# Mixture-of-experts stage on one Trainium2 core: result rows stored from ScalarE's queue, gathers left alone on GpSimd

## Chip, cores, metric

The kernel runs on one core of a Trainium2 chip, in one launch. The metric is the device time of that launch in microseconds. Engines are named as in the profile: PE (TensorE), ACT (ScalarE), DVE (VectorE), POOL (GpSimd), SP (SyncE, here only issuing DMAs).

## What is computed

Two transformer-like blocks over 512 tokens of width 1024, all in float32: first a mixer (dilated attention beside gated linear attention) and a mixture of experts, then a second mixer (pooling beside an RWKV recurrence). The change touches the mixture of experts alone, cut here to what matters:

```python
logits = xt @ router_w + router_b                 # 512 tokens, 32 experts
top_v, top_i = lax.top_k(logits, 4)
gates = softmax(top_v)
# for each expert e and the tokens that chose it (xb = their rows):
gu = xb @ w_gate_up[e] + b_gate_up[e]             # 1024 -> 2 * 1024
x_glu = minimum(gu[:, ::2], 7); x_lin = clip(gu[:, 1::2], -7, 7)
act = x_glu * sigmoid(1.702 * x_glu) * (x_lin + 1)
out = act @ w_down[e] + b_down[e]                 # 1024 -> 1024
# y[token] = sum over its 4 experts of gate * out
```

## The kernel before

The program runs in stages, one block of engine programs each, with a barrier between: `stage_front`, `mixers`, `stage_router`, `stage_experts`, `stage_second`, `stage_rwkv`. The change is in `stage_experts`.

**Units.** The tokens of each expert are cut into units of 32 rows (`SLOTS`); an expert has at least one unit. The router stage leaves a table with each unit's expert and slot code, and the count of units. Every engine walks over the units in a loop (`Fori(1, units)`), the first unit being written out ahead of it. A unit's 32 rows of 1024 lie in SBUF as 128 x 256: four quarters of the columns on four groups of 32 partitions.

**Weights.** An expert has twelve chunks of 1 MB (128 x 2048 float32), eight of gate/up and four of down. SP issues them in order of the experts (line 1653) into 18 slots (`staging`, one and a half experts). Before each it waits till the chunk that held the slot 18 earlier is used by the last unit of its expert (`free`), and after each for the landing of the one issued four before (`arrived`, which raises `chunk_in`). A quarter of each chunk is read by PE from its slot; the other three quarters are copied into a ring of four places first, chunks 2, 5, 7 and 10 by ACT (line 1785), the others by DVE (line 1853). The copies are made anew for each unit.

**PE, in each step of the loop** (lines 1767 to 1772): gate/up of unit i (`up`, eight chunks), down of unit i - 1 (`down`, four chunks), the transposes of unit i's hidden tile (`turn_hidden`, line 1736), the transposes of the gathered rows of unit i + 2 (`turn_rows`, line 1704), and the bias of unit i + 1 (line 1714).

**ACT, in each step:** three ring fills (chunks 5, 7, 10), the gate, the copy of the transposed rows (`rows_turned`), the fill of chunk 2 for the next unit, then `read_y`, which copies the down result of unit i - 1 from PSUM to `y` (line 1808) once `y_free` says that `y` was stored, and then the copy of the transposed hidden tile (`hidden_turned`, line 1796).

**POOL, in each step** (lines 1690 to 1692): `gather(i + 2)`, which reads the slot code from the table, waits till the gather before has landed (`rows_in`) and till PE has transposed the rows of unit i + 1 (`rows_ps`; the tile `rows` has a single buffer), copies the slot numbers and issues the indirect DMA (line 1676); then `store_rows(i)`, which waits for `y_read`, issues the store of `y` to DRAM (line 1683), waits for its landing and raises `y_free`. The loop is in program order, so the next gather begins after the store has landed.

The last unit's result is stored by SP (line 1660).

Of the kernel before, what the change touches and what calls it, by code (L numbers as in the profile page):

```python
# [32 lines left out]
NE, TOPK = 32, 4  # L33
# [1502 lines left out]
def stage_experts(k):  # L1536

    nc, d = k.nc, k.d
    with ExitStack() as ctx:
# [27 lines left out]
        rows_in = sem("rows_in")  # L1567
        rows_ps = sem("rows_ps")
# [10 lines left out]
        y_read = sem("expert_y_read")  # L1579
        y_out = sem("expert_y_out")  # L1580
        y_free = sem("expert_y_free")
        last_out = sem("expert_last_out")
# [35 lines left out]
        def store_of(n):  # L1618
            return d["expert_rows"][bass.ds(n, SLOTS), :].rearrange("r (c n) -> c r n", c=QUARTERS)

        with nc.Block() as block:
            @block.sync
            def _(sp):
# [34 lines left out]
                end = sp.value_load(k.table[0:1, TABLE - 2:TABLE - 1], min_val=NE - 1, max_val=NBLK - 1)  # L1658
                sp.wait_ge(y_read, end + 1)
                sp.dma_start(store_of(end * SLOTS), y[:]).then_inc(last_out, 16)  # L1660
                sp.wait_ge(last_out, 16)

            @block.gpsimd
            def _(pool):
                units = units_on(pool)
                by_quarter = d["h2"].rearrange("t (c n) -> (t c) n", c=QUARTERS)

                def gather(i, out=rows, at=0):
                    code = pool.value_load(k.table[0:1, bass.ds(i + P, 1)], min_val=0, max_val=CODES - 1)
                    if out is rows:  # L1670
                        after(pool, rows_in, 16 * i)
                        after(pool, rows_ps, i)
                    pool.tensor_copy(slot[:, at:at + 1], k.slots[:, bass.ds(code, 1)]).then_inc(slot_ready, 1)  # L1673
                    pool.wait_ge(slot_ready, i + 1)
                    pool.sem_inc(slot_seen, 1)
                    pool.indirect_dma_start(  # L1676
                        out=out[:], out_offset=None, in_=by_quarter,
                        in_offset=bass.IndirectOffsetOnAxis(ap=slot[:, at:at + 1], axis=0)).then_inc(rows_in, 16)

                def store_rows(n):  # L1680

                    pool.wait_ge(y_read, n)
                    pool.dma_start(store_of(n * SLOTS - SLOTS), y[:]).then_inc(y_out, 16)  # L1683
                    pool.wait_ge(y_out, 16 * n)
                    pool.sem_inc(y_free, 1)

                gather(0, y, 1)
                gather(1)
                gather(2)
                with pool.Fori(1, units) as i:  # L1690
                    gather(i + 2)
                    store_rows(i)
                pool.wait_ge(rows_in, 16 * units + 32)

            @block.tensor
            def _(pe):
# [3 lines left out]
                def turn_rows(i, src=rows):  # L1700
                    pe.wait_ge(rows_in, 16 * i + 16)
                    after(pe, rowsT_ready, i)
                    for b in range(2):
                        mm = pe.transpose(k.bank(6)[:, b * P:(b + 1) * P], src[:, b * P:(b + 1) * P], ident)  # L1704
                    mm.then_inc(rows_ps, 1)
# [73 lines left out]
            def _(act):  # L1779
# [25 lines left out]
                def read_y(n, done):  # L1805
                    act.wait_ge(chunk_done, done)
                    act.wait_ge(y_free, n + 1)
                    act.activation(y[:], k.bank(4)[:, 0:GLU], ACT.Copy).then_inc(y_read, 1)  # L1808

                act.sem_inc(y_free, 1)  # L1810
# [16 lines left out]
                with act.Fori(1, units) as i:  # L1827
# [7 lines left out]
                    read_y(i - 1, i * CHUNKS + CHUNKS)  # L1835
                    hidden_turned(i)
# [6 lines left out]
                read_y(end, units * CHUNKS + CHUNKS)  # L1843

# [1275 lines left out]
```

## Time and profile before

| | us |
|---|---|
| median of 3 runs | 2101.05 |
| lowest and highest | 2095.19, 2104.95 |
| the profiled execution, its own time | 2098.68 |
| its span in the profile | 2097.1 |

In that span PE is busy for 81%, DVE for 54%, ACT for 41%, POOL for 12%; 516.46 MB are moved, 246 GB/s in the mean. The expert stage is the stretch from some 368 to some 1696 us.

Busy time is the time in which an engine executes; issuing DMAs, waiting and branching are not counted. A wait is put down to what released it. PE's granted clock is written as a share of 2.4 GHz, so that 0.5 is the level of 1.2 GHz.

### The profile page before, as it was taken

The numbers are of one execution on the slowest core, as the hardware profiler recorded it, in microseconds if no ns is written. First come the engines' busy times: TensorE is split into PE (matmuls) and PEld (weight loads), VectorE is DVE, ScalarE is ACT, GpSimd is POOL, SyncE is SP. The second block draws the span as 40 slices with busy tenths as digits, with TensorE's granted clock in tenths as the row PEclk, the third lists the DMA queues.
The fourth block names the chain that finished last, engine by engine and source line by source line (L and its number), as shares of the span: only waits on it lengthen the run. The fifth ranks groups of instructions, "written<-read, shape, count | busy, mean of one in ns | idle before, by whom it ended". The sixth has DMA issues, their size and how long they took to land. (4 is left out here: it accounts for less than half of the span.)

```text
span 2097.1 us, 50062 instructions
## 1 busy us (share of the span) xinstructions
PE 1704.3 (81%) x16925; PEld 894.4 (43%) x16926; DVE 1136.5 (54%) x1698; ACT 853.6 (41%) x1131; POOL 257.8 (12%) x304
## 2 busy tenths in 40 slices
PE   6999898677977787878887787879778657999797
PEld 4999644232332332323332233323323125777763
DVE  5874536554654554545654555546545356694555
ACT  5344521543543443434543444434444234442421
POOL 0000000211111111111111111111111030151000
PEclk9999998897998888989987889889988777999999
DMA  8871840659478866995389985997598983231011
GB/s 301 277 242 33 216 190 21 260 220 423 163 305 335 336 265 259 394 381 221 137 343 404 424 337 222 371 400 302 205 415 344 417 308 80 73 91 42 4 52 40
DMA packets 135287, 516.46 MB, mean 246 GB/s; under 512 B 19927, under 2 KB 58728, under 8 KB 85929
## 3 DMA queue, kind: packets, MB, share of 16 engines
q1 hardware_dynamic: 117016, 483.74, 58.9%
q0 software_dynamic: 18048, 31.20, 4.5%
q8 instruction: 51, 0.84, 0.2%
q10 hardware_dynamic: 146, 0.48, 0.1%
q14 instruction: 26, 0.21, 0.0%
HBM read 492.44 MB, written 22.81 MB: 246 GB/s over the span
## 5 line engine op out<-in xcount | busy, mean ns | idle before, releaser
L1853 DVE COPY ring<-staging 128x1536 f32 (+1 forms) x638 | 600.5, 967 | 578.0 <-PE banks L1727 464.3
L1785 ACT ACTIVATE ring<-staging 128x1536 f32 (+1 forms) x319 | 473.8, 1487 | 731.6 <-PE banks L1727 545.9
L1727 PE MATMUL banks<-staging,rowsT 128*32 (+1 forms) x1268 | 633.5, 654 | 42.4 <-DVE ring L1853 21.3
L1727 PE MATMUL banks<-ring,rowsT 128*32 128x512 f32 x3840 | 641.9, 655 | 0.0
L1727 PEld LDWEIGHTS banks<-staging,rowsT 128*32 128x32 f32 x1268 | 140.8, 118 | 480.8 <-issue 476.6
L1750 PE MATMUL banks<-staging,hiddenT 128*32 x1280 | 294.0, 383 | 1.6 <-DVE ring L1853 1.3
L1750 PE MATMUL banks<-ring,hiddenT 128*32 128x256 f32 x3840 | 294.8, 383 | 0.0
L1704 PE MATMUL banks<-sq,rows 128*128 128x128 f32 x162 | 41.1, 343 | 234.5 <-DMA rows<-h_rows,slot 234.5
L1750 PEld LDWEIGHTS banks<-staging,hiddenT 128*32 128x32 f32 x1280 | 141.7, 111 | 153.7 <-issue 47.3
L1750 PEld LDWEIGHTS banks<-ring,hiddenT 128*32 128x32 f32 x3840 | 155.3, 111 | 0.0
L1727 PEld LDWEIGHTS banks<-ring,rowsT 128*32 128x32 f32 x3840 | 155.2, 118 | 0.0
L602 PE MATMUL banks<-w_in_hi,hT 128*128 128x256 f32 (+1 forms) x768 | 147.3, 291 | 1.5 <-issue 1.5
L1673 POOL COPY slot<-slots 128x1 int32 x82 | 30.2, 368 | 878.5 <-issue 857.8
L2196 PE MATMUL banks<-h3T,w_in_hi 128*128 128x512 f32 x400 | 129.4, 405 | 1.4 <-DVE h3T L2374 1.4
L1704 PEld LDWEIGHTS banks<-sq,rows 128*128 128x128 f32 x162 | 21.0, 165 | 245.1 <-DMA rows<-h_rows,slot 245.1
L602 PEld LDWEIGHTS banks<-w_in_hi,hT 128*128 128x128 f32 x768 | 122.5, 194 | 3.5 <-issue 3.5
L1683 POOL DMA_DIRECT2D expert_rows<-y_rows x79 | 62.8, 795 | 388.6 <-ACT y_rows L1808 365.7
L602 PE MATMUL banks<-w_in_lo,hT 128*128 128x256 f32 (+1 forms) x384 | 109.7, 286 | 0.0
L1676 POOL DMA_INDIRECT rows<-h_rows,slot x81 | 96.4, 1190 | 66.6 <-POOL slot L1673 51.0
L2196 PEld LDWEIGHTS banks<-h3T,w_in_hi 128*128 128x128 f32 x400 | 76.1, 191 | 23.1 <-issue 4.1
L2196 PE MATMUL banks<-h3T,w_in_lo 128*128 128x512 f32 x200 | 78.9, 395 | 0.0
L602 PEld LDWEIGHTS banks<-w_in_lo,hT 128*128 128x128 f32 x384 | 74.5, 194 | 1.9 <-issue 1.9
(434 smaller groups left out, 1939.2 us busy)
## 6 DMA issues: line engine op xcount, KB each, us to landing
staging<-in_w_gate_up SPq DMA_DIRECT2D x250, 1024.0 KB, 11.5
staging<-in_w_down SPq DMA_DIRECT2D x128, 1024.0 KB, 12.8
stage<-in_w_mod SPq DMA_DIRECT2D x21, 1024.0 KB, 5.8
stage<-in_w_in SPq DMA_DIRECT2D x25, 512.0 KB, 4.0
stage<-in_w_in SPq DMA_DIRECT2D x11, 1024.0 KB, 6.1
expert_rows<-y_rows POOLq DMA_DIRECT2D x79, 128.0 KB, 8.6
expert_rows<-catT SPq DMA_DIRECT2D x1, 7936.0 KB
early<-in_w_gate_up SPq DMA_DIRECT2D x6, 1024.0 KB, 12.9
```

The source lines that it names most:

```text
L602: mm = pe.matmul(k.bank(4 + t)[:, 0:w], hT[:, a, q, tt], b[:, q, :], start=(q == 0 and a == 0 and b is hi), stop=(q == KT - 1 and a == 1))
L1673: pool.tensor_copy(slot[:, at:at + 1], k.slots[:, bass.ds(code, 1)]).then_inc(slot_ready, 1)
L1676: pool.indirect_dma_start(out=out[:], out_offset=None, in_=by_quarter, in_offset=bass.IndirectOffsetOnAxis(ap=slot[:, at:at + 1], axis=0)) ...
L1683: pool.dma_start(store_of(n * SLOTS - SLOTS), y[:]).then_inc(y_out, 16)
L1704: mm = pe.transpose(k.bank(6)[:, b * P:(b + 1) * P], src[:, b * P:(b + 1) * P], ident)
L1727: mm = pe.matmul(k.bank(0)[c * SLOTS:(c + 1) * SLOTS, :], rowsT[:, q % 2, row], w, start=first and q == 0, stop=not first and q == KT - 1, ...
L1750: mm = pe.matmul(k.bank(4)[c * SLOTS:(c + 1) * SLOTS, 0:GLU], hT[:, b, m * SLOTS:(m + 1) * SLOTS], w, start=(m == 0 and b == 0), stop=(m = ...
L1785: act.activation(ring[:, pos % RING, :], staged(i, e, pos, PART, CHUNK - PART), ACT.Copy).then_inc(act_filled, 1)
L1853: dve.tensor_copy(ring[:, pos % RING, :], staged(i, e, pos, PART, CHUNK - PART)).then_inc(dve_filled, 1)
L2196: mm = pe.matmul(k.bank(n % 4), w[:, n % NW, q, :], hT[:, b, q, :], start=(q == 0 and a == 0), stop=(q == KT - 1 and a == 2))
```

## The change

The store of `y` moves from POOL to ACT: after `read_y`, ACT waits for its own copy to be written (`y_read`) and issues the store from its own DMA queue; the copy for the next unit waits for that store's landing (`y_out`). The last store too is ACT's, and SP's is removed. POOL only gathers. It waits itself for the landing of each gather and then raises `rows_here`, on which PE now waits in place of `rows_in`; then it waits for the transposes of those rows and gathers the next into the same buffer. The first two gathers, into `y` and `rows`, have a semaphore each, and the second no longer waits for the first.

```diff
--- before.py
+++ after.py
@@ -1565,6 +1565,9 @@
         slot_ready = sem("slot_ready")
         slot_seen = sem("slot_seen")
         rows_in = sem("rows_in")
+        first_in = [sem(f"first_rows{m}_in") for m in range(2)]
+        rows_here = sem("rows_here")
+        rows_free = sem("rows_free")
         rows_ps = sem("rows_ps")
         rowsT_ready = sem("rowsT_ready")
         chunk_in = sem("chunk_in")
@@ -1577,9 +1580,8 @@
         turned_ps = sem("hidden_turned_ps")
         hT_ready = sem("hiddenT_ready")
         y_read = sem("expert_y_read")
+        y_seen = sem("expert_y_seen")
         y_out = sem("expert_y_out")
-        y_free = sem("expert_y_free")
-        last_out = sem("expert_last_out")
         settled = sem("early_settled")
         gate_diff = sem("gate_diff")
         gate_exp = sem("gate_exp")
@@ -1655,42 +1657,38 @@
                     arrived(m - AHEAD)
                 for m in range(NE * CHUNKS - AHEAD, NE * CHUNKS):
                     arrived(m)
-                end = sp.value_load(k.table[0:1, TABLE - 2:TABLE - 1], min_val=NE - 1, max_val=NBLK - 1)
-                sp.wait_ge(y_read, end + 1)
-                sp.dma_start(store_of(end * SLOTS), y[:]).then_inc(last_out, 16)
-                sp.wait_ge(last_out, 16)
 
             @block.gpsimd
             def _(pool):
                 units = units_on(pool)
                 by_quarter = d["h2"].rearrange("t (c n) -> (t c) n", c=QUARTERS)
 
-                def gather(i, out=rows, at=0):
+                def gather(i, out, at, done):
                     code = pool.value_load(k.table[0:1, bass.ds(i + P, 1)], min_val=0, max_val=CODES - 1)
-                    if out is rows:
-                        after(pool, rows_in, 16 * i)
-                        after(pool, rows_ps, i)
                     pool.tensor_copy(slot[:, at:at + 1], k.slots[:, bass.ds(code, 1)]).then_inc(slot_ready, 1)
                     pool.wait_ge(slot_ready, i + 1)
                     pool.sem_inc(slot_seen, 1)
                     pool.indirect_dma_start(
                         out=out[:], out_offset=None, in_=by_quarter,
-                        in_offset=bass.IndirectOffsetOnAxis(ap=slot[:, at:at + 1], axis=0)).then_inc(rows_in, 16)
-
-                def store_rows(n):
-
-                    pool.wait_ge(y_read, n)
-                    pool.dma_start(store_of(n * SLOTS - SLOTS), y[:]).then_inc(y_out, 16)
-                    pool.wait_ge(y_out, 16 * n)
-                    pool.sem_inc(y_free, 1)
-
-                gather(0, y, 1)
-                gather(1)
-                gather(2)
+                        in_offset=bass.IndirectOffsetOnAxis(ap=slot[:, at:at + 1], axis=0)).then_inc(done, 16)
+
+                gather(0, y, 1, first_in[0])
+                gather(1, rows, 2, first_in[1])
+                pool.wait_ge(first_in[0], 16)
+                pool.sem_inc(rows_here, 1)
+                pool.wait_ge(first_in[1], 16)
+                pool.sem_inc(rows_here, 1)
+                pool.wait_ge(rows_ps, 2)
+                pool.sem_inc(rows_free, 1)
+                gather(2, rows, 0, rows_in)
                 with pool.Fori(1, units) as i:
-                    gather(i + 2)
-                    store_rows(i)
-                pool.wait_ge(rows_in, 16 * units + 32)
+                    pool.wait_ge(rows_in, 16 * i)
+                    pool.sem_inc(rows_here, 1)
+                    pool.wait_ge(rows_ps, i + 2)
+                    pool.sem_inc(rows_free, 1)
+                    gather(i + 2, rows, 0, rows_in)
+                pool.wait_ge(rows_in, 16 * units)
+                pool.sem_inc(rows_here, 1)
 
             @block.tensor
             def _(pe):
@@ -1698,7 +1696,7 @@
                 ident = k.sq[:, IDENT, :]
 
                 def turn_rows(i, src=rows):
-                    pe.wait_ge(rows_in, 16 * i + 16)
+                    pe.wait_ge(rows_here, i + 1)
                     after(pe, rowsT_ready, i)
                     for b in range(2):
                         mm = pe.transpose(k.bank(6)[:, b * P:(b + 1) * P], src[:, b * P:(b + 1) * P], ident)
@@ -1804,10 +1802,15 @@
 
                 def read_y(n, done):
                     act.wait_ge(chunk_done, done)
-                    act.wait_ge(y_free, n + 1)
+                    act.wait_ge(y_out, 16 * n + 16)
                     act.activation(y[:], k.bank(4)[:, 0:GLU], ACT.Copy).then_inc(y_read, 1)
 
-                act.sem_inc(y_free, 1)
+                def store_y(n):
+                    act.wait_ge(y_read, n + 1)
+                    act.sem_inc(y_seen, 1)
+                    act.dma_start(store_of(n * SLOTS), y[:]).then_inc(y_out, 16)
+
+                act.sem_inc(y_out, 16)
                 rows_turned(0, 0)
                 fill(0, 0, 2)
                 act.wait_ge(bias_set, 1)
@@ -1833,6 +1836,7 @@
                     rows_turned(i + 1, i * CHUNKS + KT)
                     fill(i + 1, expert_on(act, i + 1), 2)
                     read_y(i - 1, i * CHUNKS + CHUNKS)
+                    store_y(i - 1)
                     hidden_turned(i)
                 act.wait_ge(act_filled, units * len(BY_ACT) + 1)
                 act.sem_inc(act_filled, 2)
@@ -1841,6 +1845,9 @@
                 act.activation(k.gates[:], k.gates[:], ACT.Exp).then_inc(gate_exp, 1)
                 end = act.value_load(k.table[0:1, TABLE - 2:TABLE - 1], min_val=NE - 1, max_val=NBLK - 1)
                 read_y(end, units * CHUNKS + CHUNKS)
+                store_y(end)
+                act.wait_ge(y_out, 16 * units + 16)
+                act.sem_inc(y_seen, 1)
 
             @block.vector
             def _(dve):
```

How instructions stand on POOL in the loop over the units, before: the table read, slot copy and gather, followed by the store (L1683).

```order
L1690 ISA
L1669 TENSOR_LOAD table
L1669 ISA x2
L1596 ISA
L1673 ISA
L1673 COPY slot<-slots 128x1
L1674 REGISTER_ALU
L1676 DMA rows<-h_rows,slot 128x256
L1683 ISA
L1683 DMA expert_rows<-y_rows 4x32x256
L1684 REGISTER_ALU
L1690 REGISTER_ALU
```

And with the change, the same loop on POOL; L1687 is the wait for the transposes.

```order
L1684 ISA
L1687 REGISTER_ALU
L1667 ISA
L1667 TENSOR_LOAD table
L1667 ISA x2
L1668 ISA
L1668 COPY slot<-slots 128x1
L1669 REGISTER_ALU
L1671 DMA rows<-h_rows,slot 128x256
L1684 REGISTER_ALU
L1684 COMPARE_AND_BRANCH
```

The store is gone from POOL's loop, and the table read, which stood ahead of the waits, now stands behind them.

On ACT, at the end of each step of the loop, the y copy, the hiddenT copy and the branch back, before:

```order
L1808 ACTIVATE y_rows<-banks 128x256
L1796 ACTIVATE hiddenT<-banks 128x256
L1827 REGISTER_ALU
L1827 COMPARE_AND_BRANCH
L1837 ISA
```

And with the change, the same place on ACT:

```order
L1805 ISA
L1806 ACTIVATE y_rows<-banks 128x256
L1811 ISA
L1811 DMA expert_rows<-y_rows 4x32x256
L1794 ACTIVATE hiddenT<-banks 128x256
L1830 REGISTER_ALU
L1830 COMPARE_AND_BRANCH
```

The store's issue now stands between the y copy and the hiddenT copy, and the fills of the next step come behind both.

## Rows read from the trace of the kernel before

**Rows 1.** The page's 40 equal slices of the span: PE busy, DMA share, GB/s

```profile
PE   6999898677977787878887787879778657999797
...
DMA  8871840659478866995389985997598983231011
GB/s 301 277 242 33 216 190 21 260 220 423 163 305 335 336 265 259 394 381 221 137 343 404 424 337 222 371 400 302 205 415 344 417 308 80 73 91 42 4 52 40
```

**Rows 2.** Busy time by stretch of the span, engine by engine (us, instructions in brackets)

```profile
core 0: us, PE busy (x) PEld busy (x) DVE busy (x) ACT busy (x) POOL busy (x), PEclk, DMA share, GB/s
395.25:1686.69 1291.44, 1019.52 (x10587) 390.76 (x10587) 666.29 (x871) 556.30 (x632) 184.32 (x236) 0.87 0.78 314
948.09:959.60 11.51, 11.51 (x138) 4.75 (x135) 8.48 (x12) 7.05 (x9) 0.76 (x1) 1.00 1.04 414
959.60:980.44 20.84, 13.10 (x138) 5.00 (x135) 8.34 (x12) 7.03 (x9) 3.46 (x5) 0.84 0.56 224
1004.75:1016.26 11.51, 11.51 (x138) 4.75 (x134) 8.47 (x12) 7.04 (x9) 2.62 (x3) 1.00 0.08 19
1016.26:1029.07 12.81, 11.80 (x138) 4.86 (x134) 8.35 (x12) 7.04 (x9) 2.44 (x3) 1.00 0.09 24
971.00:1031.00 60.00, 58.00 (x674) 23.67 (x666) 41.98 (x55) 35.19 (x40) 11.49 (x14) 1.00 0.08 24
1143.00:1204.00 61.00, 46.06 (x488) 17.71 (x484) 32.64 (x42) 26.66 (x31) 9.67 (x12) 0.84 1.01 425
```

**Rows 3.** Waits of PE between 395 and 1687 us: total us, times, longest

```profile
PE banks L1704 <- DMA rows<-h_rows,slot: 231.6, 39, 9.6
PE banks L1727 <- DVE ring L1853: 20.0, 17, 6.0
PE banks L1727 <- ACT ring L1785: 14.1, 11, 1.9
```

**Rows 4.** Timeline of POOL, 945 to 986 us: start, us, what, idle before and releaser

```profile
950.06 0.76 POOL L1683 DMA_DIRECT2D expert_rows<-y_rows  x1 [9.70 <-ACT y_rows L1808]
959.96 0.46 POOL L1673 COPY slot<-slots 128x1 int32 x1 [9.13 <-issue]
961.24 0.99 POOL L1676 DMA_INDIRECT rows<-h_rows,slot  x1 [0.82 <-ACT y_rows L1808]
```

**Rows 5.** Timeline of PE, 947 to 971 us: hidden tile (L1736), gathered rows (L1704)

```profile
948.37 0.38 PE L1704 MATMUL banks<-sq,rows 128*128 128x128 f32 x2
...
959.60 0.44 PE L1736 MATMUL banks<-sq,glu 128*128 128x128 f32 x2
967.68 0.69 PE L1704 MATMUL banks<-sq,rows 128*128 128x128 f32 x2 [7.64 <-DMA rows<-h_rows,slot]
```

**Rows 6.** Tile y_rows, whole program: the stores' landing

```profile
DMA to landing us min/median/max: 3.7/8.6/9.9
```

**Rows 7.** Tile rows, whole program: the gathers' landing

```profile
DMA to landing us min/median/max: 2.7/6.1/7.9
```

**Rows 8.** Line 1660: the last store, issued by SP (ns min/median/max)

```profile
L1660 SPq DMA_DIRECT2D expert_rows<-y_rows x1: 774/774/774, 1694.3 to 1694.3; - x1
```

**Rows 9.** Timeline of ACT, 0 to 12 us: a DMA issue of its own

```profile
4.46 0.50 ACTq L424 DMA_DIRECT2D mod<-in_b_mod  x1
```

**Rows 10.** Timeline of SP, 0 to 12 us: issues behind each other

```profile
1.83 5.53 SPq L418 DMA_DIRECT2D stage<-in_w_mod  x3
```

**Rows 11.** Timeline of ACT, 1003 to 1018 us: y copy (L1808), ring fill (L1785)

```profile
1005.64 0.37 ACT L1808 ACTIVATE y_rows<-banks 128x256 f32<-128x256 f32 x1
...
1008.02 1.49 ACT L1785 ACTIVATE ring<-staging 128x1536 f32 x1 [1.74 <-PE banks L1727]
```

**Rows 12.** DMA queues, 1143 to 1204 us: packets, MB, share of 16 engines

```profile
q1 hardware_dynamic: 3450, 25.12, 97.7%
```

**Rows 13.** Line 1653, 395 to 1690 us: the weight transfers' landing

```profile
DMA to landing us min/median/max: 4.7/12.0/15.1
```

## The prediction

> **What bounds the kernel now.** I read the page's slices first: PE is busy nearly throughout, the DMA engines swing between 1 and 9 tenths [rows 1]. In the expert stage neither is full. So I took the stage from the first to the last transposition of a hidden tile, 395.25 to 1686.69: 1291.4 us for 79 steps from unit to unit, PE busy 1019.5, clock 0.87, DMA share 0.78 [rows 2]. A step that waits for nothing takes 11.51 us, beside idle DMA engines (share 0.08) and beside full ones (1.04) alike [rows 2]; transfers in flight do not slow PE. 79 such steps are 909.3 us, so 382 us of the stage are something else. PE's own waits name the largest part: 231.6 us in 39 waits for gathered rows, against 20.0 + 14.1 us for weight copies into the ring [rows 3]. The other 116 us are spread over the steps with waits, 3.0 us for each of the 39. One shows how: 959.60 to 980.44 is 20.84 us = 11.51 + 7.64 of wait + 1.7, at granted clock 0.84, so partly at the 1.2 GHz level after the idle time. Another waited 0.30 us and still took 12.81 at full clock [rows 2].
>
> Why the rows are late is seen on POOL [rows 4] beside PE [rows 5]. The transposes that free rows run at 948.37. POOL cannot gather: it stores the result of an older unit at 950.06, waits till that has landed (8.6 us is the median [rows 6]), loads the next slot code, copies it at 959.96 and gathers only at 961.24. PE comes at 959.60 + 0.4 and gets its transposes at 967.68, 6.4 us after the gather was issued. The wait for the store's landing stands between the event that frees the buffer and the gather.
>
> **The change, part by part.** The order excerpts show POOL's loop without the store, and ACT's with it between the y copy and the hiddenT copy.
>
> (a) Removed from POOL: the store's 0.76 us [rows 4] and the wait for its landing, 3.7 to 9.9 us with a median of 8.6 [rows 6]. The gather now follows the transposes that free rows. Its preparation (code, slot copy, issue) takes about 961.24 − (950.06 + 8.6) = 2.6 us, I take 2.7 [rows 4], landing 6.1 us in the median and 7.9 at most [rows 7]. From the transposes to landing: 2.7 + 6.1 = 8.8, at worst 10.6. PE returns to the transposes one step, 11.5 us, later. So I cost the 39 gather waits at zero: **−231.6 us of waits**, and what rode on them. The extra slack is only 0.9 us at the worst landing.
>
> (b) Relay: POOL waits for the landing and raises a semaphore for PE, one more short instruction in that slack: nothing.
>
> (c) Added to ACT, before the hiddenT copy: a wait for its own y copy and the store's issue. The nearest row is the same strided store on SP: 0.77 us [rows 8]. A plain issue on ACT took 0.50 us [rows 9], and on SP, with several megabytes outstanding, three took 5.53 us, 1.84 each [rows 10]; these are the ends. ACT's 0.50 was issued inside that stretch of SP, 1.83 to 7.36, so ACT does not stand behind SP's backlog there; I take 0.77, about 1.0 with the wait. Behind it stand the hiddenT copy (needed only a gate/up later) and the fill of chunk 5. ACT is idle 1.74 us before that fill today [rows 11]; it ends at 1009.51, and PE reaches chunk 5 at 1005.81 + 5 × 0.86 = 1010.11. That cover is 2.3 us: **nothing**. If it is gone, each us over it costs a us per step.
>
> (d) y's buffer: ACT waits for the landing of the store of the unit before, issued a step earlier. Landing from POOL is at most 9.9 us [rows 6]; from issue to the next y copy about 10.5. Nothing in the sum, but the upper end lies close.
>
> (e) The last store, from SP to ACT: the same transfer, the same wait. Nothing.
>
> **What is late next: the weights.** While transfers are always in flight, 1143 to 1204, the engines move 425 GB/s with share 1.01 [rows 2], and SP's queue of it 25.12 MB in 61 us, 412 GB/s [rows 12]. The twelve chunks of an expert, 1.05 MB each, take 30.6 us, 2.55 a chunk. The reference's router on these inputs gives the 32 experts 5, 1, 2, 5, 3, 2, 2, 3, 3, 3, 2, 2, 2, 7, 2, 2, 1, 2, 2, 3, 4, 2, 2, 2, 3, 4, 1, 2, 3, 1, 1, 1 units (80 in all; the seven-unit one is the idle DMA stretch 971 to 1031). An expert with one unit falls behind the weights by 30.6 − 11.5 = 19.1 us, one with two by 7.6; three gain 3.9, four 15.4.
>
> How far may the stream be behind before PE waits? If the last unit of an expert starts at T, the slots freed then take the last six chunks of the next expert and the first six of the one after: the first lands at T + 0.9 + 4.7 (shortest landing [rows 13]) = T + 5.6, the twelfth at T + 33.6. A two-unit expert in between frees the next slots early enough; chunk 7 of the following one lands at T + 38.7 and is copied by T + 40.2. PE needs it at T + 3 × 11.5 + 7 × 0.86 = T + 40.5. So a lag of 7.6 + 0.3 = 7.9 us costs nothing, and all over it is waited for. Carried through the list (lag never below zero, cut to 7.9 after each wait), experts up to the 31st leave 15 waits: six of 7.6, four of 7.3, two each of 11.2 and 19.1, one of 15.2, 150.6 us in sum (without the last expert, whose lag falls after the stretch).
>
> Each wait may again carry 3.0 us, 45 in sum, or nothing, where lag covers it. I take the full 45, since the steps with waits today carry that [rows 2, 3].
>
> **Sum.** New stage: 909.3 + 150.6 + 45 = 1105 us; saved 1291.4 − 1105 = 186 us. Against the profiled execution's own 2098.7 us (span 2097.1): 1912. The median shown is 2.4 us above that execution: **1915 us**. Bounds: with no clock and refill loss 1870; with a stream of 2.45 a chunk (29.4 an expert) the list gives 126.6 instead of 150.6, so 24 less.
>
> The Trainium skill ("DMA: Bandwidth & Descriptors", "Where 436 GB/s comes from") speaks against so large a gain: it says that loads from HBM are bound at about 358 GB/s per core. The trace disagrees, with 425 GB/s over 61 us [rows 2]; by the page's figure an expert would be an estimated 35.1 us, the list would give 252 us of waits, and the time would be about 2017.
>
> **The rivals.**
> A, the stream is slower than in the stretch I took, once gathers, stores and fills are denser. For it: slices of 371 to 394 GB/s [rows 1]; against it: 425 with everything running. At 381 GB/s an expert takes 33.0 us, the list gives 202: 51 more, 1966. The skill's bound above is this rival's far end. 0.07, of it 0.02 for a pace below 371.
> B, ACT's cover breaks. For it: 2.3 us against an issue that nobody has timed on ACT in this stage; SP's long issues. At 3.3 us after the copy, one over the cover, some 50 steps that do not wait for weights lose a us each: about 1965. 0.08.
> C, slower than before. ACT waits at its y copy for the store's landing while fills queue behind it, so a step lasts as long as landing plus y copy and issue, 1.1 us. Decisive once landing exceeds 1291.4 / 79 − 1.1 = 15.2 us. Against it: 9.9 at most from POOL; for it: ACT's queue shares the engines with weights and its landing under load is not in the trace. At 16 us: 79 × 17.1 = 1351, so 2161. 0.04.
> D, the gathers stay late, because the engines are full most of the time now: 2.7 + 7.9 leaves 0.9. If half the steps lost 1.3 us as the one of 12.81 did, 51 more: 1966. 0.05.
> E, the gather wait is only exchanged for weights, within 0.5% of before (10 us, about what a measurement of this kernel can tell from no change). The list would have to give over 330 us. 0.02.
>
> **How the numbers follow.** The forecast case has 0.74 and spans about 1885 to 1945. A, B and D (0.20) end near 1966; the range 1885 to 1965 takes in most of their nearer half and leaves out C, E and the far ends. Faster by over 0.5%: 0.94; within: 0.02; slower: 0.04.
>
> **What would show it.** PE's waits for gathered rows near zero; waits of PE on ring fills up from 34 to some 150 us, lying at the experts with one or two units; steps of 11.51 in a row within long experts; DMA share of the stage up from 0.78 to about 0.91, the stage near 1105 us. POOL without waits on y. ACT's idle time before chunk 5's fill down from 1.74 to about 0.7, never zero with PE waiting for that fill. The prediction is wrong if steps inside a seven-unit expert exceed 11.6 (B, C or D), or if 12 chunks take over 32 us (A).

## The result, and the profile after

The changed kernel took **1994.93 us** in the median of 4 runs (1988.23 to 1998.82), the kernel before 2098.12 on the same chip: a ratio of 0.9501, 95% interval 0.9463 to 0.9539. It is faster, as forecast, but by 103 us and not by the 186 forecast; 1995 lies above the range of 1885 to 1965. The profiled execution took 1994.18 us, its span is 1992.4.

The stage, cut as before from the first to the last transposition of a hidden tile, and four steps from unit to unit in it (columns as in [rows 2]):

```profile
393.68:1583.93 1190.25, 1004.52 (x10587) 374.40 (x10587) 667.90 (x871) 562.19 (x632) 139.99 (x158) 0.93 0.84 343
951.03:962.95 11.92, 11.72 (x139) 4.65 (x135) 8.44 (x12) 7.03 (x9) 1.81 (x2) 1.00 0.07 22
513.53:525.43 11.90, 11.72 (x138) 4.68 (x134) 7.72 (x11) 7.04 (x9) 1.82 (x2) 1.00 0.96 395
695.48:708.96 13.48, 11.72 (x139) 4.70 (x135) 8.15 (x12) 7.15 (x9) 1.82 (x2) 1.00 0.82 320
708.96:726.83 17.87, 13.36 (x139) 4.75 (x135) 8.39 (x12) 7.12 (x9) 1.82 (x2) 0.90 0.73 286
```

Against [rows 2] the stage fell from 1291.4 to 1190.2, 101 of the span's 105 us; the forecast was 1105. Two things don't fit it. The step that waits for nothing takes 11.91 us, where it took 11.51, beside idle engines too. And beside the weights steps come in pairs, here 13.48 and 17.87, 31.3 us for two, with the DMA engines less busy (share 0.82 and 0.73) than a stage that waits for weights would show.

What PE waits for, 395 to 1600 us (us in total, times, longest):

```profile
PE banks L1725 <- ACT ring L1783: 149.5, 92, 4.5
PE banks L1725 <- DVE ring L1860: 35.6, 29, 6.3
```

There is no row for gathered rows any more; in [rows 3] it had 231.6 us. But of the fills that PE now waits for, ACT's have 149.5 us and DVE's 35.6, though both draw on the same weights. So something holds ACT. The same view of ACT:

```profile
ACT y_rows L1806 <- DMA expert_rows<-y_rows: 103.9, 38, 4.2
```

ACT stands at its y copy 38 times for the landing of the store of the unit before. ACT's timeline around one of these:

```profile
514.42 0.36 ACT L1806 ACTIVATE y_rows<-banks 128x256 f32<-128x256 f32 x1
515.05 1.05 ACTq L1811 DMA_DIRECT2D expert_rows<-y_rows  x1
...
530.03 0.38 ACT L1806 ACTIVATE y_rows<-banks 128x256 f32<-128x256 f32 x1 [3.63 <-DMA expert_rows<-y_rows]
...
533.28 2.86 ACT L1783 ACTIVATE ring<-staging 128x1536 f32 x2 [1.04 <-issue]
```

The store issued at 515.05 had not landed before about 530, 15 us later, where POOL's stores needed 9.9 at most [rows 6]. The fill behind it is late, and PE waits for it:

```profile
534.90 1.05 PE L1725 MATMUL banks<-staging,rowsT 128*32 x1 [3.91 <-ACT ring L1783]
```

The step of 951.03, with the engines idle, shows the other part, on ACT and in the last line on PE:

```profile
951.91 0.36 ACT L1806 ACTIVATE y_rows<-banks 128x256 f32<-128x256 f32 x1
952.54 1.07 ACTq L1811 DMA_DIRECT2D expert_rows<-y_rows  x1
953.71 0.38 ACT L1794 ACTIVATE hiddenT<-banks 128x256 f32<-128x256 f32 x1 [1.44 <-PE banks L1725]
955.16 2.86 ACT L1783 ACTIVATE ring<-staging 128x1536 f32 x2 [1.06 <-PE banks L1725]
...
956.78 0.61 PE L1725 MATMUL banks<-staging,rowsT 128*32 x1 [0.20 <-ACT ring L1783]
```

Before, the hiddenT copy came right behind the y copy of 1005.64 [rows 11]:

```profile
1005.90 0.38 ACT L1796 ACTIVATE hiddenT<-banks 128x256 f32<-128x256 f32 x1
```

The issue takes 1.07 us, not 0.77. The hiddenT copy starts 1.80 us after the y copy instead of 0.26, and the fill of chunk 5 3.25 us after it instead of 2.38 [rows 11]. The queues of the page, before:

```profile
q0 software_dynamic: 18048, 31.20, 4.5%
q10 hardware_dynamic: 146, 0.48, 0.1%
```

and after:

```profile
q0 software_dynamic: 6672, 20.72, 2.8%
q10 hardware_dynamic: 10706, 10.96, 1.7%
```

The same stores were 144 packets each on POOL's queue, (18048 − 6672) / 79, and are 132 on ACT's, (10706 − 146) / 80. The data are 128 rows of 1 KB in both; 16 packets are over in one case and 4 in the other. If those are one for each DMA engine that takes part, ACT's queue spreads a store over 4 engines, 32 rows each, and POOL's over 16. The runs below were chosen to tell that, the long issue, and mere traffic apart. The Trainium skill ("DMA: Bandwidth & Descriptors", "Why a DMA increments its semaphore by 16") says that the number of engines is the largest up to 16 that divides the outermost dimension of both sides of the copy, with an exception for some copies issued from GpSimd; the packet counts of this case agree (128 rows on one side and 4 pieces on the other give 4). That could be worked out before the run.

### The profile page after: what moved, and what is told of

Same layout as the page of the kernel before. It is cut to its first block and busy times, and to the rows that moved or that the text cites. A ratio compares the mean times of both kernels' runs of the same rounds, so it can differ in the third digit from the quotient of the medians.

```text
span 1992.4 us, 50139 instructions
## 1 busy us (share of the span) xinstructions
PE 1685.5 (85%) x16925; PEld 875.5 (44%) x16926; DVE 1137.9 (57%) x1698; ACT 859.5 (43%) x1131; POOL 211.0 (11%) x225
## 3 DMA queue, kind: packets, MB, share of 16 engines
q0 software_dynamic: 6672, 20.72, 2.8%
q10 hardware_dynamic: 10706, 10.96, 1.7%
## 5 line engine op out<-in xcount | busy, mean ns | idle before, releaser
L1725 PE MATMUL banks<-staging,rowsT 128*32 (+1 forms) x1268 | 644.6, 649 | 188.7 <-ACT ring L1783 149.5
L1725 PE MATMUL banks<-ring,rowsT 128*32 128x512 f32 x3840 | 654.4, 650 | 0.0
L1783 ACT ACTIVATE ring<-staging 128x1536 f32 (+1 forms) x319 | 465.3, 1481 | 400.0 <-PE banks L1725 146.2
L1725 PEld LDWEIGHTS banks<-staging,rowsT 128*32 128x32 f32 x1268 | 128.8, 115 | 631.7 <-issue 626.4
L1725 PEld LDWEIGHTS banks<-ring,rowsT 128*32 128x32 f32 x3840 | 144.6, 115 | 0.0
L1668 POOL COPY slot<-slots 128x1 int32 x82 | 17.4, 212 | 1177.8 <-PE banks L1702 973.3
L1671 POOL DMA_INDIRECT rows<-h_rows,slot x81 | 126.7, 1565 | 64.8 <-POOL slot L1668 64.8
L1869 DVE TENSOR_SCALAR lin<-banks 128x256 f32<-128x256 f32 x80 | 34.0, 425 | 94.2 <-PE banks L1725 94.2
L1794 ACT ACTIVATE hiddenT<-banks 128x256 f32<-128x256 f32 x80 | 30.8, 385 | 112.9 <-PE banks L1725 100.1
L1806 ACT ACTIVATE y_rows<-banks 128x256 f32<-128x256 f32 x80 | 30.0, 375 | 106.8 <-DMA expert_rows<-y_rows 103.9
```

The source lines that it names most:

```text
L1671: pool.indirect_dma_start(out=out[:], out_offset=None, in_=by_quarter, in_offset=bass.IndirectOffsetOnAxis(ap=slot[:, at:at + 1], axis=0)) ...
L1725: mm = pe.matmul(k.bank(0)[c * SLOTS:(c + 1) * SLOTS, :], rowsT[:, q % 2, row], w, start=first and q == 0, stop=not first and q == KT - 1, ...
L1783: act.activation(ring[:, pos % RING, :], staged(i, e, pos, PART, CHUNK - PART), ACT.Copy).then_inc(act_filled, 1)
L1794: act.activation(hT[:].rearrange("p b n -> p (b n)"), k.bank(2)[:, 0:2 * P], ACT.Copy, scale=1.0 / ALPHA).then_inc(hT_ready, 1)
L1869: dve.tensor_scalar(lin[:], k.bank(0)[:, GLU:PART], LIMIT + 1.0, 1.0 - LIMIT, ALU.min, ALU.max).then_inc(lin_ready, 1)
```

## The experiments

Times are medians of four runs, of two in experiments 2, 3 and 8; ratios are to the kernel before on the same chip. "Stage" is cut as above; diffs are against the changed kernel unless said, and "..." marks what is left out of them.

**1. The result written in one contiguous piece**, its quarters in another order in memory; all else stays.

```diff
-                    act.dma_start(store_of(n * SLOTS), y[:]).then_inc(y_out, 16)
+                    act.dma_start(d["expert_rows"][bass.ds(n * SLOTS, SLOTS), :].rearrange("r (c n) -> (r c) n", c=QUARTERS),
+                                  y[:]).then_inc(y_out, 16)
```

> The changed kernel, but ACT's store writes its 128 x 256 block to 128 rows of 1 KB in a row in DRAM (the same bytes and packet size; the quarters of a token's row end up in other places, so the output is another one). Theory L (landing): the changed kernel's store has 132 packets, 128 of data and 4 that close it, where POOL's had 144, 128 and 16; so it runs on four DMA engines, lands some 15 us after its issue beside the weights, and ACT stands at the next y copy. With a destination of 128 equal rows it should have 144 packets, land in under 11 us, ACT's waits at the y copy (103.9 us) go, the time falls to 1910 to 1945. Theory I (issue): what costs is ACT's time for the issue, 1.07 us, and the sequencer's work behind it; then the 104 us of waits stay whatever the destination, and the time gains at most what a shorter issue gives, 79 x 0.4 = 32 us: 1963 or more. Theory W (weights): what is left is the weight stream; the time stays at 1990 to 2000.

Measured: 1891.91 us (1888.62 to 1892.70), ratio to before 0.9045 (0.9029 to 0.9060), below the 1910 to 1945 expected, as the shorter issue came on top. The store's issue, and the queue:

```profile
L1811 ACTq DMA_DIRECT2D expert_rows<-y_rows x80: 347/349/398, 409.0 to 1487.4; - x80
q10 hardware_dynamic: 11666, 10.97, 1.7%
```

Now 144 packets a store, an issue of 0.35 us, no wait of ACT for a landing, and steps of 11.51. The same bytes leave from the same queue: neither traffic nor ACT's queue as such is the cause. Stage and a stretch with transfers always in flight:

```profile
393.66:1480.49 1086.83, 982.34 (x10586) 374.11 (x10587) 663.27 (x871) 564.22 (x632) 140.18 (x158) 0.93 0.90 375
1000.00:1060.00 60.00, 49.49 (x458) 15.59 (x450) 30.16 (x39) 26.64 (x30) 4.94 (x6) 0.83 1.01 426
```

This is the stage of the forecast: 1086.8 against 1105, share 0.90 against 0.91, 426 GB/s against 425.

**2 and 3. No store, and a quarter of it** (32 rows of 1 KB).

```diff
-                    act.dma_start(store_of(n * SLOTS), y[:]).then_inc(y_out, 16)
+                    act.sem_inc(y_out, 16)
```
```diff
-                    act.dma_start(store_of(n * SLOTS), y[:]).then_inc(y_out, 16)
+                    act.dma_start(d["expert_rows"][bass.ds(n * SLOTS, SLOTS), 0:GLU], y[0:SLOTS, :]).then_inc(y_out, 16)
```

> The changed kernel without any store of the result rows: ACT raises the semaphore itself where it issued the store, and a store of zeros in an earlier stage covers all rows instead of two thirds of them. Leaves out: the expert outputs. L and I: both costs are gone, steps of 11.51 us in long experts, PE's waits are for weights only, the stage (last hidden tile minus first) is some 1105 us as first forecast, the time 1905 to 1925. W: no change, 1990 to 2000.

> The changed kernel with ACT storing only the first of the four quarters of the result rows (32 rows of 1 KB; zeros cover the rest). Leaves out: three quarters of the expert outputs. The issue stays on ACT, the transfer is small. L: landing under 9 us, no waits at the y copy, time 1910 to 1945, with steps of 11.5 to 11.9 us by how long the issue is. I: waits gone only if the issue is shorter; if the issue still takes 1.0 us, the time stays within 20 us of 1995. W: 1990 to 2000.

Measured: 1885.02 us, 0.9011 (0.8990 to 0.9031), stage 1069.2; and 1890.25 us, 0.9036 (0.9012 to 0.9059), stage 1075.7, issue 0.33 us. Both are faster than expected, and both are within 7 us of the full contiguous store: a store with a short issue that lands in time costs little. How little can't be read from the stages, 17.6 and 11.1 us shorter than in experiment 1: these two kernels also write more zeros earlier, and their stage begins some 12 us later (at 406 us against 394).

**4. The store back on POOL, behind the gather**, without a wait for its landing there.

```diff
...
+                def store_rows(n):
+                    pool.wait_ge(y_read, n)
+                    pool.dma_start(store_of(n * SLOTS - SLOTS), y[:]).then_inc(y_out, 16)
...
                     gather(i + 2, rows, 0, rows_in)
+                    store_rows(i)
...
-                    store_y(i - 1)
...
```

> Half of the change: POOL issues the stores again, but only ACT waits for their landing; the gather follows the store's issue. L: landing from POOL is 8.6 us, under the 10.5 us that the buffer has, so no waits at the y copy; ACT has no issue, so clean steps are 11.51. The gather is issued some 5.2 us after the transposes and lands 6.1 to 7.9 later, 11.3 to 13.1 against 11.5: beside full DMA engines it is late by up to 1.5 us, so 1930 to 1980. I: the same 11.51, and no prediction on landing. W: 1990 to 2000. If the removed wait on the landing was not what held the gather, it stays near 2098.

Measured: 2117.74 us (2115.33 to 2121.04), ratio 1.0119 (1.0100 to 1.0138), a miss. PE's waits, and POOL's timeline:

```profile
PE banks L1710 <- POOLq L1690: 194.0, 78, 12.1
```
```profile
917.51 0.76 POOL L1677 DMA_DIRECT2D expert_rows<-y_rows  x1 [12.33 <-ACT y_rows L1814]
919.45 0.19 POOL L1668 COPY slot<-slots 128x1 int32 x1 [1.18 <-PE banks L1710]
920.46 0.99 POOL L1671 DMA_INDIRECT rows<-h_rows,slot  x1 [0.82 <-POOL slot L1668]
```

L1690 is the relay that tells PE that rows have landed. It now stands behind the store, the store waits for the y copy, and so rows that are there are announced a step late. POOL waits 12.33 us for the y copy, PE 78 times for POOL. The edit made a wait of its own; it says nothing on landings.

**5. The order on POOL that avoids this**: slot code and copy as soon as the last gather has landed, the gather right behind the transposes, the store behind the gather; the relay is raised ahead of all of them, and ACT alone waits for the landing. ACT's `store_y` goes as in 4; the wait for the transposes stands in `gather`, ahead of the issue (`free`).

```diff
...
-                with pool.Fori(1, units) as i:
-                    pool.wait_ge(rows_in, 16 * i)
+                with pool.Fori(1, end) as i:
+                    pool.wait_ge(rows_in, 16 * i + 16)
                     pool.sem_inc(rows_here, 1)
-                    pool.wait_ge(rows_ps, i + 2)
-                    pool.sem_inc(rows_free, 1)
-                    gather(i + 2, rows, 0, rows_in)
+                    gather(i + 3, rows, 0, rows_in, free=i + 3)
+                    store_rows(i)
...
```

> A candidate. POOL issues both, in this order: the slot numbers of the next gather are read and copied as soon as the last gather has landed, the gather is issued right behind the transposes that free rows, the store right behind the y copy; ACT alone waits for the store's landing, and issues nothing. Theory L (a store spread over 16 engines lands in 8.6 us and costs ACT nothing): store issued some 2.4 us after the hidden tile's transposes, landed by 11, the next y copy is at 12.4; gather landed by 9. Steps of 11.51 us as with the contiguous store, PE waits for weights only: stage 1075 to 1095, time 1885 to 1900. Theory I2 (POOL's software-made transfers are slower in each other's company): landings over 10 us, waits at the y copy or for rows, over 1910.

Measured: **1902.76 us** (1900.74 to 1908.06), 0.9078 (0.9035 to 0.9121), just above the 1885 to 1900 of theory L and under the 1910 of I2. Tile y_rows:

```profile
L1680 POOL DMA_DIRECT2D expert_rows<-y_rows x80: 688/1054/1502, 412.7 to 1500.1; - x80
...
DMA to landing us min/median/max: 4.0/8.7/9.9
```

The same 4x32x256 store in the same place in memory, beside a weight stream as dense as in experiment 1 (stage 1095.9, share 0.90), lands in 9.9 us at most from POOL's queue. Of the versions that write what the reference wants, this is the fastest, 92 us ahead of the changed kernel.

**6. As 5, but the slot code and copy behind the wait for the transposes** (diff against 5).

```diff
...
-                    gather(i + 3, rows, 0, rows_in, free=i + 3)
+                    pool.wait_ge(rows_ps, i + 3)
+                    pool.sem_inc(rows_free, 1)
+                    gather(i + 3, rows, 0, rows_in)
                     store_rows(i)
...
```

> As the candidate, but the slot numbers are read and copied only after the transposes (as in the changed kernel): gather issued 3.1 us after the hidden tile's transposes, landed by 9.4 to 11; the store is issued at 4.9 and lands at 13.5 beside the weights, 1.1 us after the next y copy would begin. L: waits of ACT at the y copy of about 1 us in the steps beside full DMA engines, cover for it is under 1 us, so 1890 to 1930, not under the candidate's time.

Measured: 1907.34 us (1905.39 to 1910.65), 0.9100 (0.9056 to 0.9143). ACT waits for the landing at its y copy 39 times, 34.2 us in all, as expected, but the time can't be told apart from 5: the preparation of a gather fits into the step, as the forecast had it.

**7. As 4, but PE waits for the gather's landing itself** (diff against 4).

```diff
-                def turn_rows(i, src=rows):
-                    pe.wait_ge(rows_here, i + 1)
+                def turn_rows(i, arrived, src=rows):
+                    pe.wait_ge(*arrived)
...
-                    turn_rows(i + 2)
+                    turn_rows(i + 2, (rows_in, 16 * i + 16))
...
```

> The half change of e4 mended. In e4 the relay that told PE of a gather's landing stood behind the next store in POOL's order, which waits for the y copy, which comes after the transposes that wait for the relay; PE waited 176 us on that. Here PE waits for the landing itself. POOL issues the store, then the gather; only ACT waits for the store's landing. L: gather issued 5.2 us after the hidden tile's transposes, landed 6.1 to 7.9 later beside the weights, so late by 0 to 1.5 us in those steps and in time in the others (landing 2.8 to 3.5): 1895 to 1960. If what delays gathers is the store's transfer itself rather than the wait for its landing: over 2050.

Measured: 1917.69 us (1911.74 to 1918.18), 0.9144 (0.9099 to 0.9190). PE's waits for gathered rows:

```profile
PE banks L1710 <- DMA rows<-h_rows,slot: 2.3, 6, 0.7
```

What PE waits on turns 2117.7 into 1917.7, with POOL's program left as it is. That shows the relay as the cause of 4, and the gathers' landing as in time even when the gather stands behind the store.

**8. As 1, with half the columns of each weight chunk loaded** (the other halves keep old values).

```diff
-                    sp.dma_start(staging[:, m % STAGED * CHUNK:(m % STAGED + 1) * CHUNK],
-                                 up(e, c) if c < KT else down(e, c - KT)).then_inc(raw_in[m % STAGED], 16)
+                    size = CHUNK if m < STAGED + EARLY else CHUNK // 2
+                    sp.dma_start(staging[:, m % STAGED * CHUNK:m % STAGED * CHUNK + size],
+                                 (up(e, c) if c < KT else down(e, c - KT))[:, 0:size]).then_inc(raw_in[m % STAGED], 16)
```

> The kernel with the contiguous store (e1), in which each weight chunk beyond the first 24 brings only its first 1024 of 2048 columns (half the bytes of a chunk; the other half keeps what an earlier expert left). Leaves out: half of the later weights, and the places of the result rows. Theory W, that what is left above 11.51 us a step is the wait for the weight stream: it is gone, all steps are 11.51 but the first few, the stage is 79 x 11.51 = 909 to 920 us instead of 1087, the time 1710 to 1725. If the excess came from something else that goes with few units per expert (the register loads, the ring), it stays over 950.

Measured: 1743.93 us, 0.833 (0.8241 to 0.8420), stage 940.8. The expected 1710 to 1725 and 909 to 920 were missed. The weights are at least 146 of the 177.5 us by which the stage of experiment 1 exceeds 79 × 11.51. PE's waits for the ring fall to 10.5 us behind ACT and 6.2 behind DVE, 20 waits in all.

The rest, 31.5 us, lies mostly at single-unit experts. One of these steps:

```profile
931.30:948.62 17.32, 14.16 (x139) 4.41 (x135) 10.04 (x13) 7.66 (x9) 1.27 (x2) 0.90 0.98 363
```

The engines are full in it (0.98), at 363 GB/s instead of 425, and twelve half chunks, 6.29 MB, take 17.3 us at that pace. So this rest too looks like the weight stream, slower here than with whole chunks; no run takes that apart.

**9. Four stores, one per quarter of y**, each 32 rows at the reference's pitch of 4 KB.

```diff
-                    act.dma_start(store_of(n * SLOTS), y[:]).then_inc(y_out, 16)
+                    for c in range(QUARTERS):
+                        act.dma_start(d["expert_rows"][bass.ds(n * SLOTS, SLOTS), c * GLU:(c + 1) * GLU],
+                                      y[c * SLOTS:(c + 1) * SLOTS, :]).then_inc(y_out, 16)
...
```

> The changed kernel with the store cut into four, one for each quarter, 32 rows of 1 KB each to their proper places, all issued by ACT. L: each runs on 16 engines (36 to 48 packets), all land in under 11 us: no waits at the y copy. I: four issues of 0.33 us and the register work between them take 1.6 to 2.0 us against 1.07 of the one store, so clean steps are 12.2 to 12.9 instead of 11.91, hidden where PE waits for weights. Both together: 1910 to 1960. If the y copy still waits 104 us, the number of engines is not what sets the landing.

Measured: 1928.72 us (1926.55 to 1930.83), 0.9208 (0.9165 to 0.9252), stage 1120.4. The issue and the queue:

```profile
L1812 ACTq DMA_DIRECT2D expert_rows<-y_rows x320: 321/322/802, 409.2 to 1525.9; - x160
q10 hardware_dynamic: 15506, 10.98, 1.8%
```

The destination is the strided one of the change, with 48 packets a piece, 32 rows and 16 over, and ACT never waits for a landing: the stride isn't the cause. Four issues, 1.29 us, make the clean step 12.39.

**10 and 11. Other splits of one store, made only by the shape of the destination**: 8x16x256, then 2x64x256 (the rows land in another order).

```diff
-                    act.dma_start(store_of(n * SLOTS), y[:]).then_inc(y_out, 16)
+                    act.dma_start(d["expert_rows"][bass.ds(n * SLOTS, SLOTS), :].rearrange("(r t) n -> r (t n)", t=2)
+                                  .rearrange("r (a n) -> a r n", a=8), y[:]).then_inc(y_out, 16)
```
```diff
-                    act.dma_start(store_of(n * SLOTS), y[:]).then_inc(y_out, 16)
+                    act.dma_start(d["expert_rows"][bass.ds(n * SLOTS, SLOTS), :].rearrange("r (h a n) -> a (r h) n", h=2, a=2),
+                                  y[:]).then_inc(y_out, 16)
```

> The changed kernel with ACT's store written as 8 pieces of 16 rows of 1 KB at other places of the same 128 KB (the output is another one). If the engines are as many as the outermost dimension of the transfer, as 132 = 128 + 4 packets say of the four pieces and 144 = 128 + 16 of the contiguous one, this has 136 packets and 16 rows per engine. The changed kernel's 32 rows per engine landed after 14.9 us beside the weights, 0.46 us a row; so 7.5 us here: no waits at the y copy. The issue tells the second thing: if it is 1.07 us as for four pieces, clean steps stay at 11.91 and the time is 1905 to 1925; if it is 0.35 as for the contiguous one, 11.51 and 1885 to 1900.

> As e10, with 2 pieces of 64 rows: 130 packets, 64 rows per engine, beside the weights 64 x 0.46 = 29.6 us to landing. ACT then stands at the y copy till some 30 us after the last one while weights flow, so steps of about 30 us there, and clean steps without weights: slower than the changed kernel by over 60 us and perhaps than the kernel before, 2060 to 2350. If the landing does not follow the rows per engine, the time stays at 1990 or below.

Measured, 10: 1925.99 us (1923.73 to 1933.09), 0.9216 (0.9178 to 0.9254), just above what was expected; stage 1117.4. Its queue and issue:

```profile
q10 hardware_dynamic: 11026, 10.96, 1.7%
L1811 ACTq DMA_DIRECT2D expert_rows<-y_rows x80: 1107/1132/1239, 409.7 to 1521.2; - x80
```

Measured, 11: **2232.27 us** (2224.46 to 2238.41), 1.0677 (1.0629 to 1.0725), slower than the kernel before; stage 1419.7:

```profile
q10 hardware_dynamic: 10546, 10.96, 1.5%
L1811 ACTq DMA_DIRECT2D expert_rows<-y_rows x80: 1027/1053/1172, 407.9 to 1825.5; - x80
ACT y_rows L1806 <- DMA expert_rows<-y_rows: 328.1, 43, 14.6
```

and one of its stores on ACT's timeline:

```profile
702.17 1.04 ACTq L1811 DMA_DIRECT2D expert_rows<-y_rows  x1
...
728.03 0.38 ACT L1806 ACTIVATE y_rows<-banks 128x256 f32<-128x256 f32 x1 [14.53 <-DMA expert_rows<-y_rows]
```

136 packets and 130: 8 over and 2 over. The first three stores of the table have an issue of 1.05 to 1.13 us and differ in that number. For each run one store was taken that goes out beside full DMA engines (share 1.02 or 1.03), in the window that holds all its packets: 706.78 to 727.75 us in experiment 11, 703.5 to 713.9 in the changed kernel, 697.99 to 703.75 in 10, 700.1 to 703.4 in 1.

```profile
q10 hardware_dynamic: 130, 0.13, 1.8%
q10 hardware_dynamic: 132, 0.13, 3.6%
q10 hardware_dynamic: 136, 0.13, 6.5%
q10 hardware_dynamic: 144, 0.13, 11.4%
```

| store | packets | first packet to last | issue to last packet | ACT's waits for it | stage |
|---|---|---|---|---|---|
| 2x64x256 (11) | 130 | 21.0 us | 25.6 us (issued 702.17) | 328.1 us, 43 | 1419.7 |
| 4x32x256 (the change) | 132 | 10.4 us | 15.3 us (issued 698.58) | 103.9 us, 38 | 1190.2 |
| 8x16x256 (10) | 136 | 5.8 us | 9.6 us (issued 694.19) | none | 1117.4 |
| contiguous (1), short issue | 144 | 3.3 us | 6.8 us (issued 696.61) | none | 1086.8 |

Each doubling of the packets that are over about halves the transfer, as it would if they count the engines and the rows of one engine go out one behind the other: 64 rows in 21.0 us and 32 in 10.4, 0.33 us a row. Bytes, queue and the number of rows are the same, and the issue costs the same in the first three.

The DMA view of the changed kernel, 526.5 to 530 us, the end of the landing shown above (the first row is the busy tenths of the 16 engines in 40 slices):

```profile
DMA  2022222222222222222222222224022402422222
...
q1 hardware_dynamic: 48, 0.33, 22.2%
q10 hardware_dynamic: 42, 0.04, 3.2%
```

22.2 + 3.2 = 25.4% of 16 engines is the work of 4. Nearly every slice stands at 2 tenths, so some four engines still work, sending 42 rows of the store and 48 packets of weights, about one for one, while the other twelve are done: a row of 1 KB costs its engine the turn of a weight packet as well, 3.5 us × 4 / 42 = 0.33 us a row. And the weights' share on those four engines is late with it, which fits the lower DMA share of the stage (0.84 against 0.90 in experiment 1).

## Why the prediction was wrong

**Right: step (a).** The 231.6 us of waits for rows are gone to nothing, and experiment 7 leaves 2.3 us of them even with the store ahead of the gather's turn. **Right: step (b)** for the relay where the change puts it; experiment 4 shows its price one place later, behind a wait: 194.0 us.

**Right in size, the weights.** The stage of experiment 1, where no store is late, is 1086.8 us against the forecast's 909.3 + 150.6 + 45 = 1105, and experiment 8 ties 146 us of it to the stream. The stream was not slower than assumed (426 GB/s), so rival A falls. The 358 GB/s of the Trainium skill ("DMA: Bandwidth & Descriptors", "Where 436 GB/s comes from") is given there as one core's half of 716 GB/s; here one core ran alone and was not held to it. The list of lags also fits step by step. Of the 79 steps of experiment 1, 59 take 11.51 or 11.52 us, and 15 exceed 11.51 by 7.4 to 18.6 us, 167.1 in sum, where the list had 15 waits of 7.3 to 19.1, 150.6 in sum; five more exceed it by some 2 us. What was too high is the 45 us on top: the long steps carry 1.1 us each beyond the list, not 3.0. PE's own waits for the ring are only 58.2 + 44.9 = 103.1 us, several to a long step; the other 74 us (177.5 − 103.1) ride on them or beside them.

**Wrong: step (d), "landing from POOL is at most 9.9 us".** This is the step that failed. It priced the landing from ACT's queue by the row of POOL's queue, for the same rows and bytes. On ACT's queue it took 15 us beside the weights, more than the 10.5 that the prediction had between issue and next y copy. ACT then stands at the y copy (103.9 us, 38 times), its fills are late, and PE waits behind them; part of the weights is late beside it. From 132 packets to 136, 4 engines to 8, with nothing else changed but the destination's shape, the stage goes from 1190.2 to 1117.4: **73 us** (the issue is 0.06 us longer there, so this is if anything too little).

The price could have been seen. The kernel before has one such store on a hardware queue, its last one, on SP: the very row that step (c) took for the issue [rows 8]. Its packets stand alone in the DMA view of before, 1694 to 1698 us:

```profile
DMA  0000000000000000023221222232222222000000
...
q1 hardware_dynamic: 132, 0.13, 11.0%
```

These are 132 packets and not POOL's 144, with some 2 tenths of the 16 engines at work. The risk itself was named (rival C).

**Wrong in size: step (c), the issue and its cover.** The issue took 1.07 us instead of 0.77, and with the wait for the y copy 1.54 us were added ahead of the hiddenT copy (1.80 − 0.26), not 1.0. That is still under the cover of 2.3 us, and yet the clean step lost 0.40 us, 11.91 against 11.51. The cover was less than worked out: it counted all of ACT's 1.74 us of idle time before the fill of chunk 5 [rows 11], but 1.06 us of it stay between the hiddenT copy and that fill, and at 533.28, where they are 1.04, the profile names nothing that ACT waits for. So the fill starts 0.87 us later than before and ends at 955.16 + 1.49 = 956.65, while PE, whose first chunk starts at 952.08, reaches chunk 5 at 952.08 + 5 × 0.86 = 956.38. The prediction's own sign, steps over 11.6 us inside the seven-unit expert, came true with the 11.92 at 951.03. Rival B had the direction, with 3.3 us added and one us a step lost. From experiment 10 (1.13 us) to 1 (0.35 us) the stage goes from 1117.4 to 1086.8: **31 us**, which is 79 × 0.39. The engines go from 8 to 16 there too, so this is an upper bound for the issue, though ACT waits for no landing in either. Experiment 9 stays with 16 engines and has a clean step of 12.39; its stage is 34 us over that of experiment 1.

The two add to 104 us. The stage without both lies 18 us under the forecast of 1105, so the change came out 85 us above it: 1190. The two mechanisms that ran together had 0.08 (B) and 0.04 (C) of the chance. C's mechanism came true, but not its outcome: with landings near 15 us, where 15.2 was called decisive for "slower", the kernel lost 73 us and kept the rest of its gain. C had every step last as long as a landing. In fact 38 steps of the changed kernel wait, and those beside idle engines don't: in experiment 11, with landings up to 25.6 us, C's rule would give 79 × 26.7 = 2109 us of stage, and it was 1419.7. That a long landing can make the change slower than before is shown there all the same (2232 us). Rivals D and E fell: no wait for rows, and a gain of 5%.

Still open: why the issue of 0.77 us on SP [rows 8] is 1.07 on ACT. Also open is how much of the 73 us is ACT standing at the y copy and how much is the weights' own lateness on the four engines; no run here parts them.

## What to carry to other kernels

A store that moves to another engine's queue is not the same transfer. Count the packets of its shape on a queue of the new kind (here the kernel before had one on SP), or write it so that it is one contiguous run of many rows, before its landing is priced by the old queue's row; and where the next use of its buffer is a step later, compare that landing with the step beside full engines, not with the median. When an issue is put among an engine's short copies, price it by its own shape on its own engine, and ask which fill behind it has less than that in hand. A relay that tells others of an arrival must never stand behind a wait for something else.

## What was not expected of the hardware

- One copy of 128 rows of 1 KB has its last packet 25.6, 15.3, 9.6 or 6.8 us after its issue beside a saturated weight stream, by its shape alone, with 2, 4, 8 or 16 packets over the 128. The 4x32x256 copy has 4 over on ACT's and SP's queues and 16 on POOL's.
- Its issue on ACT takes 0.35 us in contiguous form, 0.32 for 32 strided rows, and 1.05 to 1.13 in three dimensions; on POOL 0.76 before and 1.05 in experiment 5.
- With one core at work the DMA engines moved 426 GB/s over 60 us, above the 358 per core of the Trainium skill ("DMA: Bandwidth & Descriptors", "Where 436 GB/s comes from"), which halves 716 GB/s between two cores.
